# A decoder step with paged attention: the key page slices for partitions 64 to 127 are issued by ScalarE instead of SyncE

## The reference

```
kp = cache_k[o][page_table].reshape(Bs, past, 2 * H_C, HD_C)   # 8 sequences x 32 pages of 128 keys
vp = cache_v[o][page_table].reshape(Bs, past, H_C, 2 * HD_C)
s_p = einsum('bqhd,bkhd->bhqk', q, kp) * scale                 # q: 4 new tokens of each sequence
s_n = einsum('bqhd,bkhd->bhqk', q, k) * scale                  # the 4 new keys, causal
p = softmax(concatenate([s_p, s_n]))                           # 16 heads in 8 pairs
a = p[:, :, 0] - lam * p[:, :, 1]
out = a[..., :P] @ vp + a[..., P:] @ v
```

## Time and profile before

| what | before |
|---|---|
| median of three runs | 2922.7 us |
| the profiled execution | 2932.32 us |
| its span, first to last instruction | 2930.7 us |
| mean granted TensorE clock over the span | 0.899 |
| busy: PE, DVE, ACT, POOL | 2387.4, 1523.6, 670.7, 543.7 us |
| DMA queues: q1, q0, q10 | 395.54, 130.04, 8.82 MB |

### The profile page before, as it was taken

How to read it: one execution, slowest core, us unless ns; L and a number is a source line. 1 busy time by engine, 2 the same in 40 slices (tenths; PEclk the granted TensorE clock), 3 DMA queues, 4 the chain that set the end, 5 groups by cost and what they waited for, 6 DMA issues and landing times.

```text
span 2930.7 us, 44854 instructions
## 1 busy us (share of the span) xinstructions
PE 2387.4 (81%) x15136; PEld 1789.1 (61%) x15136; DVE 1523.6 (52%) x2401; ACT 670.7 (23%) x1767; POOL 543.7 (19%) x487
## 2 busy tenths in 40 slices
PE   8999999999859997999999983666657565656668
PEld 6889888988747774787888871322323232323347
DVE  5565643233246665324344326666667666657643
ACT  4122211111123333223111122222222122222221
POOL 4332432234000000002223200211111111111121
PEclk9999999999969999999999997878777777777779
DMA  5223322232177889223343349999999999999963
GB/s 168 80 81 102 104 84 78 80 118 81 65 188 235 272 273 298 89 86 104 94 127 92 110 130 254 294 282 288 289 276 289 263 267 277 280 267 274 276 196 115
DMA packets 443172, 536.70 MB, mean 183 GB/s; under 512 B 41365, under 2 KB 385314, under 8 KB 439754
## 3 DMA queue, kind: packets, MB, share of 16 engines
q1 hardware_dynamic: 404258, 395.54, 48.5%
q0 software_dynamic: 35712, 130.04, 14.6%
q10 hardware_dynamic: 3016, 8.82, 0.8%
HBM read 432.92 MB, written 101.22 MB: 182 GB/s over the span
## 4 chain that ended last, share of the span: by engine, by line
PE 56%; SPq 20%; DMA 10%; DVE 6%; issue 6%; ACT 1%; POOL 0%; POOLq 0%; ACTq 0%; DVEq 0%
SPq L2669 16%; DMA at_kp<-in_cache_k 8%; PE p_col L571 4%; PE p_col L573 4%; PE p_col L572 4%; PE p_gm L2274 4%; PE p_gm L2276 4%; PE p_gm L2275 4%; PE p_row L612 4%; PE p_row L614 3%; PE p_row L613 3%; SPq L2659 3%; PE oa_out L1832 2%; PE oa_out L1834 2%; PE oa_out L1833 2%
## 5 line engine op out<-in xcount | busy, mean ns | idle before, releaser
L3044 DVE STREAM_TRANSPOSE at_kT<-at_kp 128x1024 f32<-128x1024 f32 x256 | 315.3, 1240 | 280.0 <-DMA at_kp<-in_cache_k 263.3
L2832 PE MATMUL at_ssc<-at_kT,at_qz 128*32 128x256 f32 x2048 | 177.1, 505 | 224.8 <-DVE at_kT L3044 168.7
L2679 POOL DMA_DIRECT2D at_vp<-in_cache_v x248 | 132.6, 535 | 932.0 <-issue 925.7
L2832 PEld LDWEIGHTS at_ssc<-at_kT,at_qz 128*32 128x32 f32 x2048 | 77.5, 138 | 340.4 <-DVE at_kT L3044 210.3
L571 PE MATMUL p_col<-h_hi,p_wqk 128*128 128x352 f32 x768 | 251.3, 327 | 1.1 <-DVEq L800 1.1
L573 PE MATMUL p_col<-h_hi,p_wqk 128*128 128x352 f32 x768 | 247.1, 322 | 0.0
L572 PE MATMUL p_col<-h_lo,p_wqk 128*128 128x352 f32 x768 | 246.9, 321 | 0.0
L612 PE MATMUL p_row<-p_wvz,h_hi 128*128 128x512 f32 x512 | 203.7, 398 | 3.5 <-ACT p_vst L695 3.5
L2274 PE MATMUL p_gm<-p_whl,h_hi 128*128 128x512 f32 x512 | 203.1, 397 | 0.9 <-DVE h_lo L2411 0.6
L614 PE MATMUL p_row<-p_wvz,h_lo 128*128 128x512 f32 x512 | 202.0, 394 | 0.0
L613 PE MATMUL p_row<-p_wvz,h_hi 128*128 128x512 f32 x512 | 201.2, 393 | 0.0
(11 more groups left out here) (409 smaller groups left out, 4624.4 us busy)
## 6 DMA issues: line engine op xcount, KB each, us to landing
at_kp<-in_cache_k SPq DMA_DIRECT2D x1024, 128.0 KB, 8.1
at_vp<-in_cache_v POOLq DMA_DIRECT2D x248, 512.0 KB, 9.4
s_qk<-p_res SPq DMA_DIRECT2D x32, 528.0 KB, 2.8
p_wst<-in_w_in_a SPq DMA_DIRECT2D x32, 512.0 KB, 4.0
p_wst<-in_w_in_a SPq DMA_DIRECT2D x64, 256.0 KB, 2.9
mx_qk<-s_qk SPq DMA_DIRECT2D x16, 1024.0 KB, 9.2
p_wst<-in_w_in_c SPq DMA_DIRECT2D x64, 256.0 KB, 4.6
s_v<-p_vst SPq DMA_DIRECT2D x64, 128.0 KB, 2.9
```

What stands on the lines that cost most here:

```text
L2832: last = pe.matmul(ssc[at:at + 32, 0:2 * PAGE], qz[:, n // NGB, e, x // 2, x % 2, :], keys, start=x == 0, stop=x == 3)
L3044: dve.transpose(kT[:, n % 2, k, :], kp[n % 2][k][:]).then_inc(keys_turned, 1)
```

## The change

ScalarE issues slices 2 and 3 of every key page, those for partitions 64 to 127; SyncE keeps slices 0 and 1. Both engines read the page number for themselves and both wait for `keys_turned`. Group 0's upper slices are issued by ScalarE behind block 6 of the last projection head, group 1's ahead of step 0, and of later groups pages 0 and 1 at the end of step s (for group s + 2), pages 2 and 3 at the start of step s (for group s + 1). Value pages: as before, SyncE issues those of groups 0 and 1, GpSimd the rest.

```diff
@@ project_layer1, scalar, new(part)
                 elif part == 4:
+                    act.wait_ge(w_taken, 2 * HC - 2)
+                    act.wait_ge(few_used, 2 * HC)
+                    nxt.load_high_keys(act)
                     act.wait_ge(rows_stored[0], 16 * ROWS_STORES * (HC // 2))
@@ attend
+    LOW, HIGH = (0, 1), (2, 3)
...
-        def key(sp, n, k):
+        def key(eng, n, k, slices):
             if n >= 2:
-                sp.wait_ge(keys_turned, GP * (n - 2) + k + 1)
-            number = page_of(sp, n, k)
+                eng.wait_ge(keys_turned, GP * (n - 2) + k + 1)
+            number = page_of(eng, n, k)
...
-            for x in range(4):
+            for x in slices:
...
         def load_keys(sp):
             sp.wait_ge(s_pt, 16)
             for k in range(GP):
-                key(sp, 0, k)
+                key(sp, 0, k, LOW)
+
+        def load_high_keys(act):
+            act.wait_ge(s_pt, 16)
+            for k in range(GP):
+                key(act, 0, k, HIGH)
...
         def load_pages(sp):
-            for n, ring_of in ((1, key), (0, value)):
-                for k in range(GP):
-                    ring_of(sp, n, k)
+            for k in range(GP):
+                key(sp, 1, k, LOW)
+            for k in range(GP):
+                value(sp, 0, k)
@@ attend, sync
             for k in range(GP):
-                key(sp, 2, k)
+                key(sp, 2, k, LOW)
...
                 if s + 2 < NG:
                     for k in range(GP):
-                        key(sp, s + 2, k)
+                        key(sp, s + 2, k, LOW)
@@ attend, scalar
             turn_last()
+            for k in range(GP):
+                key(act, 1, k, HIGH)
             for s in range(LAST):
+                if s >= 1 and s + 1 < NG:
+                    for k in (2, 3):
+                        key(act, s + 1, k, HIGH)
                 if rows_at(s):
                     page_exps(s - 2)
...
                 if pick_at(s) is not None:
                     take_pick(pick_at(s))
+                if s + 2 < NG:
+                    for k in (0, 1):
+                        key(act, s + 2, k, HIGH)
                 if s == LEAVE:
                     act.drain().then_inc(c.left[4], 1)
```

More of the change, by code:

```diff
@@ L2659, in page_of @@
             return eng.value_load(at, min_val=0, max_val=N_POOL - 1)
-        def key(sp, n, k):
+        def key(eng, n, k, slices):
             if n >= 2:
-                sp.wait_ge(keys_turned, GP * (n - 2) + k + 1)
-            number = page_of(sp, n, k)
+                eng.wait_ge(keys_turned, GP * (n - 2) + k + 1)
+            number = page_of(eng, n, k)
             rows = g["cache_k"][0, bass.ds(number, 1)].rearrange("a (y i) h d -> i (a y) (h d)", i=32)
-            for x in range(4):
+            for x in slices:
                 part = slice(32 * x, 32 * x + 32)
-                sp.dma_start(kp[n % 2][k][part, :].rearrange("i (y c) -> i y c", y=KB), rows[:, :, 256 * x:256 * x + 256]).then_inc(
+                eng.dma_start(kp[n % 2][k][part, :].rearrange("i (y c) -> i y c", y=KB), rows[:, :, 256 * x:256 * x + 256]).then_inc(
                     k_loaded[n % 2 * GP + k], 16)
@@ L3171, in attend @@
         progs = Programs(sync, tensor, scalar, gpsimd, vector)
+        progs.load_high_keys = load_high_keys
         progs.load_tables, progs.load_keys, progs.load_new, progs.load_head, progs.load_pages = load_tables, load_keys, load_new, load_head, load_pages
```

## The result

The changed kernel takes 2889.53 us in the median of four runs (2883.8 to 2895.58); the kernel before, run beside it, took 2928.97. The ratio is 0.987, with a 95% interval of 0.9827 to 0.9914. The gain of 39 us, where 100 were forecast, is clear of zero, but at 1.3% it is smaller than the 2% from which a kernel is called faster here. The profiled execution took 2883.8 us, its span 2882.1 at a mean granted clock of 0.907.

A forecast was written before the change was run, and what follows sets the result against it. Late key pages, from issue and transfer, were taken to bound the attention stage: 15.76 us a step falling to 14.2 over 58 steps saves 90 us, plus 10 at the head, giving 2823 us; range 2750 to 2960.

The forecast's parts named there:

- Key waits go: Attention stage, steady part: VectorE's waits for key pages fall from 243 us to under 60.
- ScalarE comes onto the path: Attention steps: ScalarE's burst is 3.0 us too long for the 3.3 us of cover in an undisturbed step.
- the term of 13.4 us: Attention step with ScalarE in the loop: between 14.6 us at 8 key tiles and 12.6 at one.
- the 14.2 forecast with everything: Attention step in all: 13.4 us with ScalarE in the loop, 0.5 stalls, 0.3 head loads.
- 0.3 us a step: SyncE's queue: head loads and a store every eighth step hold up the lower slices, 0.3 us a step.
- The burst: ScalarE, behind the take-out: eight slices and four page-number loads a step, in effect one burst of 6.3 us.
- Stalls of ScalarE's issues: ScalarE's slice issues held before a full queue: 0.5 us a step, bounds none to 3.2.
- Page scores: TensorE's page scores in the loop of a 6-tile step: 1.93 us.
- The head of the stage: Start of the attention stage: net -10 us, bounds 0 and -20; GpSimd's first value page under way before 1825.
- Transfers at 309 GB/s: Attention stage: a 14.2 us step needs 4.39 MB at 309 GB/s, 11% over today, taken as reached.
- The 2867 that the prediction worked out for 296 GB/s: By the skill's 6% rule for two DMAs: step 14.8 us, profiled about 2867; rival "halves gain little" had 0.15.
- The second, ScalarE caught before a full queue: Rival, chance 0.25: stalls on ScalarE delay page exponentials and the whole step; 2979 us, over 3,150 at twice the surplus.

The follow-up runs named there:

- e11: The changed kernel with merge_exps and take_pick moved behind the next step's row exponentials, so the burst follows the take-out directly; 2835.6 us.
- e10: e4 with merge_exps and take_pick deferred behind the next row exponentials, and a head's store and loads spread over three steps; 2831.6 us.
- e3: The kernel before with one line changed: SyncE issues each page's slices in the order 0, 2, 1, 3; 2879.2 us.
- e6: The kernel before with four unused page-number reads added on ScalarE at the end of each step; 2929.7 us.
- e4: The changed kernel with ScalarE's slices spread: page 0 behind row exponentials, page 1 ahead of take-out, pages 2 and 3 behind it, before batch work; 2807.9 us.
- e1: The changed kernel with all eight ScalarE slices of group s + 2 right behind the take-out, ahead of take_new, merge_exps and take_pick; 2845.4 us.
- e8: The changed kernel with slices 0 and 2 on SyncE, 1 and 3 on ScalarE, so each queue alternates between partition halves; 2890.4 us.
- e7: e4 with slices 0 and 2 on SyncE, 1 and 3 on ScalarE, so each queue alternates between partition halves; 2872.5 us.

## Why the prediction was wrong

The sign and the mechanism were right, and the size was off by more than half. By its own steps:

**Key waits go: right**, and more than forecast: under 60 us were expected, 0.8 came. **ScalarE comes onto the path: right.** The signs on the page scores, the maxima and the issue's median of 0.328 us are all there; the sign of 300 GB/s or more is not (291).

**The failed step** is the term of 13.4 us for a step with ScalarE in the loop, at its premise: "in effect one burst of 6.3 us right behind the take-out of the output". The loop was worked out on a 6-tile step, where that holds: forecast 13.8 us, measured 12.8. It holds in 43 of 58 steps (in seven of these the short copy of `take_new` stands in between, 1.1 us), which take 13.80 us against the 14.2 forecast with everything (43 x -0.40 = -17 us). In the other 15, `merge_exps` or `take_pick` stands between take-out and burst with a wait of its own, and these take 18.86: 15 x 4.66 = +70 us. Together 53 us: the steady part's whole miss. The prediction took "the end of the step" for one place, though the order written out in the kernel has two more calls there; one of them stands in the description ahead of the prediction ("every eighth step it also issues two small DMAs").

e11 takes those calls out of that place and comes to 2836, 13 us from the forecast of 2823. It wins back 46 of the 70 us. The other 24 stay in the 7-tile steps, at 17.4 us, where keys are late (29 us in all): SyncE issues their lower slices behind a head's transfers, and in e10, which moves these, the 7-tile steps' key waits all but go. The prediction put that at 0.3 us a step, 17 us over the steady part, and the 7-tile steps of e11 are 8 x 3.2 = 26 us over the forecast's 14.2. That e11 lands so near is in part luck, since its 43 other steps are 0.25 us shorter than the forecast, 11 us together.

**The burst** was put at 6.3 us; from take-out to page exponentials it is 6.0 (2182.41 to 2188.38 in e11's timeline). **Stalls of ScalarE's issues** 0.5 us a step, measured 0.4. **Page scores** were put at 1.93 us from the earlier trace rows. That row was a fast one: in the kernel before they took 2.75 us in the mean of the steady part, and 3.38 one step earlier, behind an idle time (the fence of step 28 above). In the kernel after TensorE sits idle ahead of them in nearly every step, and they take 3.42 (198.6 us in 58 steps). The value sums are shorter in return. TensorE's timeline of the kernel after in step 30, and the busy times of these two pieces:

```profile
2220.86 3.22 PE L2842 MATMUL at_ssc<-at_kT,at_qz 128*32 128x256 f32 x32 [8.55 <-ACT at_alpha L2914]
...
2225.52 1.58 PE L2812 MATMUL at_ring<-at_vr,at_pT 128*128 128x128 f32 x12 [0.41 <-DVE at_pT L3134]
```

```profile
2220.80:2224.10 3.30, 3.24 (x33) 1.64 (x34) 0.00 (x0) 1.90 (x4) 0.00 (x0) 0.59 1.04 326
2225.50:2227.10 1.60, 1.58 (x14) 1.48 (x14) 1.56 (x3) 0.08 (x1) 0.00 (x0) 1.00 1.07 325
```

And the same for the pieces of the earlier trace rows in the kernel before:

```profile
2211.30:2213.20 1.90, 1.90 (x37) 0.95 (x33) 1.73 (x7) 0.00 (x0) 0.57 (x2) 1.00 0.94 251
2219.00:2221.60 2.60, 2.50 (x12) 2.31 (x12) 2.53 (x4) 0.19 (x1) 0.00 (x0) 0.50 1.01 363
```

The granted clock explains both: the scores ran at 1.00 before and at 0.59 now, mostly the lower level of 1.2 GHz, behind 8.6 us without work; the value sums ran at 0.50 before, behind a short idle, and at 1.00 now, so that 12 matmuls took 1.58 us where 10 had taken 2.48. In these steps that is +1.3 and -0.9 us; in the mean it is +1.5 for the scores (3.42 against 1.93) and -1.1 for the value sums of a 6-tile step (1.35 against 2.48). The two errors nearly cancel, which is luck: the prediction took both times as fixed.

**The head of the stage**: -10 forecast; step 6 begins 8.2 us earlier. GpSimd's first value page left at 1826.5, so the sign given (before 1825) was missed by 1.5 us. The projection's wait behind the first burst is where it was put, though larger (the burst issued from 1749.40, the block's work at 1755.03 instead of 1751.55). The stage's start moved 3.9 us, not 1.6, but in e3 and e6, which have no burst there, the stage begins at 1753.9 and 1760.7, so one trace of each can't tell the 3.9 from spread:

```profile
1749.40 5.53 ACTq L2673 DMA_DIRECT2D at_kp<-in_cache_k  x8
1755.03 0.28 ACT L2351 ACTIVATE p_sig<-p_gm 128x128 f32<-128x128 f32 x1 [5.89 <-issue]
```

**Transfers at 309 GB/s** were never tried by the changed kernel, which needs 291 at its own pace; e4 reached 316, so the term was sound. The rule that spoke against it, in the Trainium skill, SBUF — State Buffer, section "Can I just issue two DMAs to hit both halves?", puts such a pair 6% above one DMA. Here keys alone went from 228 to 288 GB/s (+26%) when each queue kept one half, and the measurement decides.

**Rivals.** The 2867 that the prediction worked out for 296 GB/s is the nearest number to the profiled 2883.8, but for another reason: e1, e4 and e11 keep the halves and the transfers as they are, and are faster by 44 to 82 us. The second, ScalarE caught before a full queue, fell in the changed kernel (22 us in all) and in e8, with the halves mixed (27 us). It came in e7 (150 us), where the halves are mixed and ScalarE's order allows a step of 13.9 us (e4) instead of 15.1. So what spared the change is not the split by halves alone: at its own pace the queues stay short either way.

**Where the expected gain went**, then: of the 100 us, 48 are there between the profiled executions, and the two calls ahead of the burst hold 45 to 54 more (e11). e4 is a further 28 us below e11: there the burst is split into lots that lie under other waits.

## What to carry to other kernels

Where a burst of DMA issues is moved to an engine that computes, price it by its worst place in the period, not by a typical step: list every call that stands between the work before and the burst, and each wait inside these. Put such issues in small lots where the engine would wait anyway; the same eight slices cost 28 us less so than in one burst with nothing ahead of it (e4 against e11), and 82 less than in the changed kernel. And before a second engine is given issues, try the order in the queue there is: here one line brought as much as the second engine.

## What the runs showed that was not expected

- Slices of one queue to lower and upper partitions in turn (e3) move keys at 256 GB/s, two of the same half in a row at 228.
- Two queues each on a half of its own give 288 to 295 GB/s; two queues with halves mixed, 257 to 261, hardly more than one queue in that order. Each of these rates is from one stretch of 4 to 6 us.
- TensorE took 3.22 us for 32 matmuls of the page scores behind an idle time of 8.6 us, and 1.93 in the earlier trace rows. They were granted 0.59 and 1.00 of the clock. Meanwhile the mean granted clock of the steady part rose, from 0.78 to 0.81.
- A DMA share of 1.05 stood beside 279, 291 and 316 GB/s in three kernels; it does not tell whether more can be moved.
